# Rotary queries of a two-block transformer kernel: the half-turn made by VectorE in pieces of 32 rows instead of a TensorE product

## The reference, cut to what matters

```
def _rope(x, cos, sin):
    x1, x2 = jnp.split(x.astype(jnp.float32), 2, axis=-1)
    return jnp.concatenate([x1 * cos - x2 * sin, x2 * cos + x1 * sin], axis=-1).astype(x.dtype)
...
    q_pe = _rope(_rmsnorm(q_pe, qpe_w), cos[None, :, None, :], sin[None, :, None, :])
    k_pe = _rope(_rmsnorm(k_pe, kpe_w), cos[None], sin[None])
...
        s = (jnp.einsum('bqhd,bkhd->bhqk', qn_b, k_nope)
             + jnp.einsum('bqhr,bkr->bhqk', qp_b, k_pe))
```

## Time and profile before

| | before |
|---|---|
| median of 3 runs | 1303.23 us (1302.95 to 1306.06) |
| profiled execution, its own time | 1303.55 us |
| its span in the trace | 1301.8 us |
| TensorE busy | 1270.6 us, 98% |
| VectorE busy | 740.0 us, 57% |
| GpSimd busy | 624.4 us, 48% |
| ScalarE busy | 470.7 us, 36% |
| mean granted TensorE clock | 0.996 of full |

### The profile page before, as it was taken

How to read it: one execution, slowest core, us unless ns; L and a number is a source line. 1 busy time by engine, 2 the same in 40 slices (tenths; PEclk the granted TensorE clock), 3 DMA queues, 4 the chain that set the end, 5 groups by cost and what they waited for, 6 DMA issues and landing times.

```text
span 1301.8 us, 20101 instructions
## 1 busy us (share of the span) xinstructions
PE 1270.6 (98%) x6790; PEld 1038.1 (80%) x6790; DVE 740.0 (57%) x1401; ACT 470.7 (36%) x1027; POOL 624.4 (48%) x416
## 2 busy tenths in 40 slices
PE   7999999999999999999999999999999999999998
PEld 6877777778788888888888878888878788888876
DVE  5236877566774545442224778778644566555541
ACT  3232333412422222221113556566302455555521
POOL 5423333247454444345563153443357777777721
PEclk9999999999999999999999999999999999999999
DMA  6413222233242333323333211111133322222212
GB/s 181 110 42 97 75 71 65 65 98 92 73 124 84 96 97 93 100 77 101 97 98 98 65 53 45 48 37 44 50 95 94 93 77 78 77 77 77 65 46 84
DMA packets 196755, 105.42 MB, mean 81 GB/s; under 512 B 19174, under 2 KB 194636, under 8 KB 196700
## 3 DMA queue, kind: packets, MB, share of 16 engines
q1 hardware_dynamic: 196252, 104.00, 28.2%
q0 software_dynamic: 432, 0.69, 0.3%
q10 hardware_dynamic: 16, 0.00, 0.0%
HBM read 102.57 MB, written 2.10 MB: 80 GB/s over the span
## 4 chain that ended last, share of the span: by engine, by line
PE 88%; DVE 5%; POOL 2%; ACT 2%; issue 2%; DMA 1%; DVEq 0%; SPq 0%; ACTq 0%; POOLq 0%
PE ps L387 21%; PE ps L388 20%; PE ps L389 20%; PE ps L418 8%; PE ps L1394 1%; POOL w_low L366 1%; PE ps L1425 1%; PE ps L1405 1%; PE ps L1157 1%; PE ps L400 1%; PE ps L401 1%; PE ps L404 1%; PE ps L971 1%; PE ps L1149 1%; PE ps L993 1%
## 5 line engine op out<-in xcount | busy, mean ns | idle before, releaser
L366 POOL TENSOR_TENSOR w_low<-w_raw,w_high 128x1024 fp32r<-128x1024 f32 x180 | 440.3, 2448 | 472.9 <-DVE w_high L361 467.7
L387 PE MATMUL ps<-h_high,w_high 128*128 128x512 f32 x816 | 332.2, 407 | 1.6 <-ACT root L1963 0.8
L388 PE MATMUL ps<-h_low,w_high 128*128 128x512 f32 x816 | 322.8, 396 | 0.0
L389 PE MATMUL ps<-h_high,w_low 128*128 128x512 f32 x816 | 321.8, 394 | 0.0
L361 DVE CAST w_high<-w_raw 128x1024 fp32r<-128x1024 f32 x183 | 155.4, 851 | 108.1 <-DMA w_raw<-in_w_in_dram 37.7
L387 PEld LDWEIGHTS ps<-h_high,w_high 128*128 128x128 f32 x816 | 153.7, 188 | 42.1 <-issue 5.7
L389 PEld LDWEIGHTS ps<-h_high,w_low 128*128 128x128 f32 x816 | 153.7, 188 | 35.1
L388 PEld LDWEIGHTS ps<-h_low,w_high 128*128 128x128 f32 x816 | 153.7, 188 | 33.9 <-issue 2.6
L1692 ACT ACTIVATE z<-ps,cv 128x512 f32<-128x512 f32 x42 | 32.7, 778 | 147.0 <-PE ps L389 146.9
L2294 DVE SCALAR_TENSOR_TENSOR z<-ps,cv,z 128x511 f32<-128x511 f32 x42 | 31.5, 749 | 91.4 <-ACT z L1692 91.4
L389 PE MATMUL ps<-m_high,w_low 128*128 128x512 f32 x176 | 69.4, 395 | 0.0
(11 more groups left out here) (373 smaller groups left out, 2411.8 us busy)
## 6 DMA issues: line engine op xcount, KB each, us to landing
w_raw<-in_w_in_dram SPq DMA_DIRECT2D x150, 256.0 KB, 3.2
w_raw<-in_w_up_dram SPq DMA_DIRECT2D x88, 256.0 KB, 3.1
w_raw<-in_w_out_dram SPq DMA_DIRECT2D x44, 256.0 KB, 3.0
w_raw<-in_w_down_dram SPq DMA_DIRECT2D x32, 256.0 KB, 3.0
w_raw<-in_w_down_dram SPq DMA_DIRECT2D x16, 192.0 KB, 2.6
rel<-in_rel_bias_dram SPq DMA_DIRECT2D x16, 192.0 KB, 2.9
x_tok<-in_x_dram SPq DMA_DIRECT2D x4, 512.0 KB, 5.3
w_raw<-in_w_ob_dram SPq DMA_DIRECT2D x8, 256.0 KB, 2.9
```

The source lines that it names most:

```text
L366: pool.tensor_tensor(w_low[:, n % RING, :], w_raw[:, n % RAW, :], w_high[:, n % RING, :].bitcast(F32), ALU.subtract).then_inc(low_made, 1)
L387: pe.matmul(acc, wh, mh, start=first and k == 0, stop=False)
L388: pe.matmul(acc, wh, ml, start=False, stop=False)
L389: done = pe.matmul(acc, wl, mh, start=False, stop=last and k == tiles - 1)
```

## The change

For the queries the product with `rot` goes. VectorE instead makes four products of 32 rows: it reads rows b to b+31 of `q_pe` and of `sin`, and writes to the rows of the other half (b XOR 32). For the signs, rows 32 to 63 and 96 to 127 of `sin` are multiplied by -1 once, in the prologue. The keys still go through `rot`; as `sin` now carries a sign there, their last sum is made in four pieces of 32 rows, with a subtraction in two. TensorE's projection that overwrites the PSUM bank (`m_project` 3) waited for VectorE to have read the rotated product, and now waits for ScalarE to have read the sums.

```diff
@@ TensorE, m_project
-                        pe.wait_ge(s["qr_part"], i * 3 + (3 * (c // 2) + 1))
+                        pe.wait_ge(s["p_root"], i * 10 + (heads(c, 6, 4) + 1))
@@ TensorE, removed with its two calls (prologue and head_then_even)
-            def m_rotate(i, c):
-                if c % 2:
-                    return
-                pe.wait_ge(s["p_normed"], i * 5 + (heads(c, 3, 2) + 1))
-                pe.matmul(ps[:, 7, :], rot[:], q_pe, start=True, stop=True).then_inc(s["qr_turned"], 1)
@@ VectorE, m_rope
                 turned = sq[:, 1, 0:S]
                 if part == 0:
-                    dve.wait_ge(s["qr_turned"], i + (c // 2 + 1))
-                    dve.tensor_tensor(tiles(turned), tiles(ps[:, 7, :]), by_columns(sin[:, META:L]), ALU.mult).then_inc(s["qr_part"], 1)
+                    dve.wait_ge(s["p_normed"], i * 5 + (heads(c, 3, 2) + 1))
+                    if c:
+                        dve.wait_ge(s["p_sum"], i * 5 + (heads(c, 3, 2) + 2))
+                    for b in (0, 32, 64, 96):
+                        src, dst = slice(b, b + 32), slice(b ^ 32, (b ^ 32) + 32)
+                        r = dve.tensor_tensor(tiles(turned[dst, :]), tiles(q_pe[src, :]), by_columns(sin[src, META:L]),
+                                              ALU.mult)
+                    r.then_inc(s["qr_part"], 1)
                     return
+                dve.wait_ge(s["qr_part"], i * 3 + (3 * (c // 2) + 1))
@@ VectorE, prologue, before m_normed(0, 0, 0)
+            dve.wait_ge(s["tables_in"], 32)
+            for b in (32, 96):
+                dve.tensor_scalar(sin[b:b + 32, :], sin[b:b + 32, :], -1.0, None, ALU.mult).then_inc(s["sin_signed"], 1)
             m_normed(0, 0, 0)
+            dve.wait_ge(s["sin_signed"], 2)
@@ VectorE, prologue, the keys
-            dve.tensor_tensor(k_pe, kpe_root, kpe_sq, ALU.add).then_inc(s["pe_part"], 1)
+            for b in (0, 32, 64, 96):
+                p = dve.tensor_tensor(k_pe[b:b + 32, :], kpe_root[b:b + 32, :], kpe_sq[b:b + 32, :],
+                                      ALU.subtract if b & 32 else ALU.add)
+            p.then_inc(s["pe_part"], 1)
```

More of the change, by code:

```diff
@@ L440, in program @@
             pe_part pe_turned tables_in
-            pe_split twice_in p_made p_kept01 p_sq01 p_sq2 p_kept2 p_sum p_root p_normed x_high x_low xp_low qr_turned qr_part
+            pe_split twice_in p_made p_kept01 p_sq01 p_sq2 p_kept2 p_sum p_root p_normed x_high x_low xp_low sin_signed qr_part
             mv_cleared mv_kept mv_turned mv_high_ mv_low_ mg_part mg_done
@@ L1259, in head_then_even @@
                 m_scores(i, c, 2)
-                m_rotate(i, c + 1)
                 m_turn(i, c, 1)
@@ L1349, in _ @@
             kpe_rows(0, 5)
-            m_rotate(0, 0)
             kpe_rows(5, KT)
```

## The result

The changed kernel takes 1322.78 us (median of 4 runs, 1321.01 to 1322.93), against 1303.11 us for the kernel before on the same chip (4 runs, 1302.95 to 1306.06): a ratio of 1.0139, 95% interval 1.0127 to 1.0152. It is slower by 19.7 us. The profiled run took 1322.77 us, with a span of 1321.1 us, 19.3 us more than before.

A forecast was written before the change was run, and what follows sets the result against it. TensorE, busy 98% of the span, was taken to bound the kernel, with VectorE as late behind the removed product. Loop +8.3, prologue +5.8 and clock +3.4 made +17.5 us on 1303.55, so 1321.0 us, range 1312 to 1327.

The forecast's parts named there:

- What bounds the kernel: TensorE busy 98% of the span, but right behind the removed product VectorE is as late, with 0.3 us of slack.
- The price of a piece: VectorE's 32-row products in the loop: 1.05 us each whatever the rows, 4.2 us for four.
- Whether pieces overlap: The four pieces in the loop: 4.2 us without overlap, 3.9 us at a pitch of 0.97.
- The loop: Three turns, VectorE 2.76 us late in each with nothing given back: +8.3 us, or +7.2 at a pitch of 0.97.
- The prologue: Keys' copy and L1119 late, +3.5 us, and four-piece sum of the keys, +2.3: +5.8 us, +3.4 without GpSimd's part.
- The clock: TensorE's five new waits: two followed by a slower clock at 1.7 us each, +3.4 us, bounds 0 and 8.5.
- Terms 4 to 6: Loop +8.3, prologue +5.8 and clock +3.4, together +17.5 us.
- VectorE having room: Rival: the pieces are hidden on VectorE and TensorE's 3.5 us are gained, 1299.8 us; chance 0.04.
- Pieces that cost by rows: Rival: a quarter of the rows takes a quarter of the time, four about 1.2 us, total about 1303; chance 0.03.
- A time without GpSimd's part and without falls: Rival: loop +7.2 or +8.3, prologue +3.4, no fall of the clock: 1314 to 1315 us; chance 0.22.
- A fall after nearly every wait: Rival: the clock falls after nearly all five waits, 1326 us, up to 1329 with another GpSimd collision; chance 0.16.
- given back later: Rival: part of the delay is given back in a later wait VectorE had anyway, 1307 to 1312 us; chance 0.06.

The follow-up runs named there:

- e3: Changed kernel with the four products with the rotation matrix put back on TensorE, their results unread: 1321.32 us, ratio 1.0139.
- e4: Changed kernel with one VectorE product of 128 rows in place of the four of 32, half-turn left out: 1303.58 us, ratio 0.9996.
- e9: Changed kernel with the four products cut by columns (128 rows, 128 columns each) instead of by rows, half-turn left out: 1306.19 us in its single run.
- e5: Changed kernel with products of a zero matrix filling TensorE's new waits in loop and prologue: 1318.47 us, ratio 1.0103.
- e10: Changed kernel with the two sign changes of the table moved ahead of the scaling of the keys' latent part: 1320.11 us, ratio 1.0127.
- e1: Changed kernel with the prologue of before, so the four pieces stand in the loop alone: 1314.04 us, ratio 1.0075.
- e6: Changed kernel with three gate-product steps moved into TensorE's wait in even heads, and ScalarE's root before its rotary copy: 1321.93 us, ratio 1.0138.

## Why the prediction was right, point by point

1. **What bounds the kernel.** Right. The place right behind the removed product decided; e3 shows that the product's time was worth nothing there, and e4 that one product on VectorE instead of four makes a gain of 0.6 us a turn out of the loss.
2. **The price of a piece.** Right: 1.04 us (said 1.05), four in 4.21 (said 4.2). e9 shows what the trace of before could not, that columns cost and rows don't. My "1.05 ns for a column" was read from dense instructions; in the strided view of the table it is (1.04 - 0.38) / 384, about 1.7 ns.
3. **Whether pieces overlap.** I took a pitch of 1.05 against 0.97. In the trace the pieces are 1.06 us apart and the norm of the keys starts 4.24 behind the first. The Trainium skill ("VectorE: DVE Perf Modes", section "Two Vector instructions with no wait between them") states, as a model, that an instruction which starts in another group of 32 rows than the one before it begins only when all earlier ones have finished. The trace agrees: with another group of 32 rows each time there is no overlap, while e9's four, which all start in the same rows, overlap by about 0.09 us each.
4. **The loop.** Said 3 x 2.76; it is 3 x 2.78 at full clock (e5, and the third turn of the changed kernel).
5. **The prologue.** Said +5.8; it is +5.23 at full clock. (Up to the product with `cos` eight instructions stand where three did, and not six: one row of the list of the change is three pieces. The sum had all eight.) Its two parts: TensorE's L1119 came 3.2 us later against the cast (said 3.5, with GpSimd at 2.4 where the collision cost 2.51 - 0.42 = 2.1), and the four-piece sum took 3.98 instead of 1.85 us, +2.1 (said 2.3). That GpSimd stops VectorE was an assumption there; e10 shows it, with a different instruction in the place. The Trainium skill ("SBUF — State Buffer", section "SBUF: two separate sides") says that VectorE and GpSimd share a pair of ports as an exclusive lock, held for a whole instruction; the trace agrees, since the piece of 3.07 us ends at 738.1, after GpSimd's L366 at 737.2, with 0.9 us of its own left.
6. **The clock.** I took two falls of five at 1.7 us, 3.4. There were four, and they cost 3.9 us together, about 1.0 each: 0.7 and 1.1 in the loop, 2.1 for the two in the prologue. Both factors were off, and they nearly cancelled. That is luck: e10 had one fall in the same five places, e1 one in three.
7. **The rest.** Terms 4 to 6 measure 8.3 + 5.2 + 3.9 = 17.5 us, as the sum said. The span grew by 19.3 and the medians by 19.7. The missing 2 us stand in no term. In this execution they lie in the neighbourhood attention, whose code is unchanged: TensorE waits 3.9 us there (L1443) where the earlier trace rows has 2.99 (L1451 before), and then runs longer at 1.2 GHz (the wait, and the window behind it):

```profile
PE ps L1443 <- DVE scaled L2635: 3.9, 1, 3.9
```

```profile
1043.60:1053.60 10.00, 6.11 (x34) 4.70 (x30) 6.10 (x13) 2.66 (x8) 5.19 (x3) 0.66 0.49 128
```

What ended the wait was VectorE, and not GpSimd as in the earlier trace rows: its five instructions of one line (L2638, L2645 in the changed kernel) took 2.53 us before and 6.78 us here. The first row is of the kernel before, the other two are of the changed one:

```profile
1022.56 2.53 DVE L2638 SCALAR_TENSOR_TENSOR nk_n<-nk_f,cv,root 128x80 f32<-128x80 f32 x5 [2.06 <-ACT root L1968]
...
1039.68 6.78 DVE L2645 SCALAR_TENSOR_TENSOR nk_n<-nk_f,cv,root 128x80 f32<-128x80 f32 x5 [2.06 <-ACT root L1960]
...
1042.75 3.71 DVE L2645 SCALAR_TENSOR_TENSOR nk_n<-nk_f,cv,root 128x16 f32<-128x16 f32 x1
```

Before, the two of the shape of the last row took 0.40 and 0.45 us; here the one of 3.71 us lies beside two GpSimd instructions and ends at 1046.46 with the second of them (L770, 1046.44). So part of the 2 us looks like one more collision with GpSimd, away from the change; in e10, whose tail is nearly as long, the wait is 3.0 us and only the clock is lower for longer. The tails in the table go from 348.1 to 350.8 us with one code, and don't follow the size of the change (e1 has 348.1, e4 349.8). Whether the changed kernel's tail is longer on the whole or only in this execution stays open; one profile for each kernel can't tell it.

The rivals fell as follows. VectorE having room would have needed 0.3 us of delay and got 2.8. Pieces that cost by rows are out by the 1.04 us. A time without GpSimd's part and without falls (1314 to 1315) did not come: both were there. Without the falls alone it is 1318.5 (e5). A fall after nearly every wait did happen in number, at a lower price than I gave it. Nothing was given back later: a turn at full clock is 2.78 us longer for a delay of 2.76, and e6 shows the delay going on through VectorE, ScalarE and GpSimd when TensorE's wait at `m_weigh` is filled.

## What to carry to other kernels

Before taking work from the busiest engine, look at which engine the chain runs on right behind it: here one product on VectorE gained 0.6 us a turn, and the split into four laid 3.4 us on an engine that was busy 57% on average but had 0.3 us of room in that place. Count a VectorE instruction by its columns and their stride and not by its rows (here 1.04 us for 512 strided columns with 32 rows as with 128), so that a split by rows multiplies its cost; and put a constant table in the order in which it is read, which took 0.36 us from each product and gave the only kernel here that was faster than both (0.998, 0.997 to 0.999). Put short VectorE work where it does not collide with GpSimd, but ask which instruction moves into the place that it leaves.

## What the runs showed that I had not expected

- **The length of a wait does not decide whether the clock falls.** The same 2.8 us before `m_weigh` was followed by a fall in turns 1 and 2 of the changed kernel and not in turn 3; in e1 in turn 3 alone. Before the first scores, waits of 3.42 us (e3), 3.54 (e4) and 3.55 (e9) were followed by means of 0.50, 0.67 and 0.66 over the next 5 or 6 us, and one of 3.41 (e10) by 1.00. With the gaps filled (e5) there was no fall in the stage. The four falls counted here are those of one execution; that another has as many is not shown.
- **A fall costs less than the stretch suggests.** The stretch of 802.00 to 807.40 at a mean of 0.68 cost turn 1 about 1.1 us, and not (1 - 0.68) x 5.4 = 1.7. Where the difference lies is not shown; it may be that VectorE's work is as late there as TensorE's.
- **The stride of one operand costs half again:** 1.05 against 0.69 us for 512 columns, with 128 rows or with 32.
